# Two heads' retention projections as seven block products over half of the depth, woven into the attention projections, and a last slab that closes in two half banks

## What is computed

```
h = rms_norm(x);  p = h @ w_in                    # per head: retention q,k,v,gate and attention q,k,v
A = silu(gate) * group_norm(retention(rot(q), rot(k), v))         # 8 heads of 128
B = softmax(rms(q) @ rms(k).T + rel_bias) @ v                     # 8 heads of 128, chunk mask
x = x + concat(A, B) @ w_out
x = x + square(relu(rms_norm(x) @ w_ff1)) @ w_ff2
```

## Time and profile before

| | |
|---|---|
| median of 3 runs | 1113.13 us (1112.95 to 1113.15) |
| profiled execution: time / span | 1113.28 / 1111.2 us |
| busy: PE, PE weight loads | 1105.2 us (99%), 942.2 us (85%) |
| busy: DVE, ACT, POOL | 830.8 us (75%), 657.3 us (59%), 51.5 us (5%) |
| granted PE clock in 40 slices | 9 tenths or more in every slice |
| DMA | 253.14 MB, mean 228 GB/s |

### The profile page before, as it was taken

One profiled execution on the slowest core, in us unless ns is written; L12 is line 12 of the kernel. 1 busy time (PEld: TensorE's weight loads), 2 busy tenths in 40 slices (PEclk: granted clock), 3 DMA queues, 4 the chain that ended last, 5 costly groups with the idle time before them and its releaser, 6 DMA issues.

```text
span 1111.2 us, 13678 instructions
## 1 busy us (share of the span) xinstructions
PE 1105.2 (99%) x5234; PEld 942.2 (85%) x5234; DVE 830.8 (75%) x828; ACT 657.3 (59%) x765; POOL 51.5 (5%) x58
## 2 busy tenths in 40 slices
PE   9999999999999999999999999999999999999998
PEld 8889899899898888888888888888888888888887
DVE  6667566576576668869787869787869787869783
ACT  6544544554554556677655577665577665577662
POOL 0100000000000000000000000000000000000000
PEclk9999999999999999999999999999999999999999
DMA  9855455454464556787797787797787797787792
GB/s 362 319 191 180 151 198 179 151 197 153 156 217 152 204 208 182 266 278 220 246 290 222 258 277 221 243 291 221 259 279 220 244 291 221 259 277 219 246 278 86
DMA packets 39551, 253.14 MB, mean 228 GB/s; under 512 B 4432, under 2 KB 4944, under 8 KB 12624
## 3 DMA queue, kind: packets, MB, share of 16 engines
q1 hardware_dynamic: 34464, 218.12, 53.4%
q0 software_dynamic: 4608, 33.56, 16.0%
q10 hardware_dynamic: 432, 0.81, 0.2%
HBM read 250.37 MB, written 2.10 MB: 227 GB/s over the span
## 4 chain that ended last, share of the span: by engine, by line
PE 99%; DMA 0%; ACT 0%; DVE 0%; ACTq 0%; issue 0%
PE acc L489 11%; PE acc L496 11%; PE acc L503 11%; PE acc L667 10%; PE acc L665 10%; PE acc L663 10%; PE bankC L643 4%; PE acc L643 4%; PE acc L638 4%; PE bankC L638 4%; PE bankC L636 4%; PE acc L636 4%; PE bankD L643 1%; PE bankD L638 1%; PE bankD L636 1%; PE acc L687 1%
## 5 line engine op out<-in xcount | busy, mean ns | idle before, releaser
L1311 DVE TENSOR_TENSOR w_lo<-raw,w_hi 128x2048 fp32r<-128x2048 f32 x180 | 410.9, 2289 | 126.8 <-ACT w_hi L924 126.6
L924 ACT ACTIVATE w_hi<-raw 128x2048 fp32r<-128x2048 f32 x180 | 344.8, 1917 | 220.8 <-PE acc L667 145.9
L1118 DVE TENSOR_TENSOR w_lo<-raw,w_hi 128x1024 fp32r<-128x1024 f32 (+1 forms) x152 | 167.8, 1107 | 68.6 <-ACT w_hi L767 68.5
L767 ACT ACTIVATE w_hi<-raw 128x1024 fp32r<-128x1024 f32 (+1 forms) x152 | 142.9, 962 | 34.3 <-PE acc L503 25.3
L489 PE MATMUL acc<-w_hi,hT_hi 128*128 128x512 f32 (+1 forms) x512 | 129.5, 374 | 0.8 <-ACT w_hi L767 0.8
L496 PE MATMUL acc<-w_hi,hT_lo 128*128 128x512 f32 (+1 forms) x512 | 123.5, 362 | 0.0
L503 PE MATMUL acc<-w_lo,hT_hi 128*128 128x512 f32 (+1 forms) x512 | 123.2, 362 | 0.0
L496 PEld LDWEIGHTS acc<-w_hi,hT_lo 128*128 128x128 f32 x512 | 93.5, 188 | 10.5
L503 PEld LDWEIGHTS acc<-w_lo,hT_hi 128*128 128x128 f32 x512 | 93.4, 188 | 10.0
L663 PE MATMUL acc<-w_hi,hF_hi 128*128 128x512 f32 x256 | 100.8, 394 | 0.0
L663 PE MATMUL acc<-w_hi,dF_hi 128*128 128x512 f32 x256 | 99.9, 390 | 0.0
(11 more groups left out here) (187 smaller groups left out, 1573.4 us busy)
## 6 DMA issues: line engine op xcount, KB each, us to landing
raw<-in_w_up SPq DMA_DIRECT2D x64, 1024.0 KB, 6.4
raw<-in_w_down SPq DMA_DIRECT2D x64, 1024.0 KB, 6.5
raw<-in_w_ret SPq DMA_DIRECT2D x32, 1024.0 KB, 4.7
raw<-in_w_att SPq DMA_DIRECT2D x28, 768.0 KB, 4.4
raw<-in_w_out SPq DMA_DIRECT2D x16, 1024.0 KB, 4.7
raw<-in_w_up POOLq DMA_DIRECT2D x16, 1024.0 KB, 8.6
raw<-in_w_down POOLq DMA_DIRECT2D x16, 1024.0 KB, 8.9
raw<-in_w_att SPq DMA_DIRECT2D x6, 384.0 KB, 7.7
```

Source lines behind the costliest of these rows:

```text
L767: nc.scalar.activation(piece(w_hi, q, 0, PIECE_KT * n), raw[:, q // 2, (q % 2) * PIECE_KT * n:(q % 2 + 1) * PIECE_KT * n], ACT.Copy).then_ ...
L924: nc.scalar.activation(w_hi[:, ring(s)], raw[:, r, :], ACT.Copy).then_inc(slab_hi, 1)
L1118: nc.vector.tensor_tensor(piece(w_lo, q, 0, PIECE_KT * n), raw[:, q // 2, (q % 2) * PIECE_KT * n:(q % 2 + 1) * PIECE_KT * n], piece(w_hi, ...
L1311: nc.vector.tensor_tensor(w_lo[:, ring(s)], raw[:, r, :], w_hi[:, ring(s)].bitcast(f32), ALU.subtract).then_inc(slab_lo, 1)
```

## The change

**Projections.** The 16 groups become four blocks of two heads. A block has 19 steps of two pieces, in this order; `I` and `J` are the plain attention slabs of the two heads, the others are retention:

```diff
+STEPS = "I0 I1 I2 I3 J0 Q1 J1 P5 J2 P6 J3 P7 P3 Z1 Q2 Z2 P4 H1 H2".split()
+LOADS = "I0 I1 I2 I3 J0 a J1 b J2 d J3 Z1 e Z2 H1 H2".split()
```

```diff
+            def s_block(b):
+                nc.vector.tensor_tensor(s_blk[:, b, :]..., hT_hi[...], hT_lo[...], ALU.add).then_inc(s_blk_ok, 1)
...
+            at_piece(0, 8, s_first)
+            at_piece(0, 8, s_second)
+            at_piece(0, 9, s_third)
+            at_piece(0, 10, s_lo, 0)
+            at_piece(0, 11, s_lo, 1)
+            at_piece(0, 13, s_lo, 2)
+            at_piece(0, 15, s_lo, 3)
```

The weight combinations are made in every block: DVE adds slab b, and later d, to slot a, and POOL's accumulating DMAs add one more slab to b and to a. Banks are seeded from `in_p5`, `in_q1` and `bX`:

```diff
+            def in_sum(i, other, read):
+                nc.vector.tensor_tensor(raw[:, r, :], raw[:, r, :], raw[:, o[0], :], ALU.add).then_inc(in_summed, 1)
+            def set_z(i):
+                nc.vector.tensor_tensor(bZ[:], in_p5[:], bX[:], ALU.subtract).then_inc(z_set, 1)
+            def set_w(i):
+                dve.wait_ge(y_set, i + 1)
+                nc.vector.tensor_tensor(bW[:], in_p5[:], bX[:], ALU.subtract).then_inc(w_set, 1)
...
+                elif step == "Z1" and m == 1:
+                    pe.wait_ge(w_set, i + 1)
```

The small work gets new places (DVE's and PE's lists, cut; `h` is the even head of the block, `u` the even retention head; the odd retention head's work stands at pieces 1 to 7 of the next block, where `ret_work` had it):

```diff
+                at_piece(i, 10, att_mean_squares, h)
+                at_piece(i, 10, in_sum, i, "b", "Q1")
+                at_piece(i, 11, att_norm, h)
+                at_piece(i, 14, in_sum, i, "d", "P5")
+                at_piece(i, 20, set_z, i)
+                at_piece(i, 24, set_w, i)
+                at_piece(i, 24, att_mean_squares, h + 1)
+                at_piece(i, 25, att_norm, h + 1)
+                at_piece(i, 33, ret_rotate, u)
+                at_piece(i, 34, ret_rotated, u)
...
+                for h, first in ((2 * i, 12), (2 * i + 1, 26)):
+                    at_piece(i, first, att_T, h)
+                    at_piece(i, (18, 30)[h % 2], att_PT, h)
+                at_piece(i, 34, ret_T, 2 * i)
```

**Last slab.** In place of two banks of 512 columns, the second is closed in halves, the right one in `bX`:

```diff
+                for m, bank, first, end in ((0, bH, 0, N), (1, bY, 0, half), (1, bX, half, N)):
...
+                    right = xs[:, 1, c * N + half:(c + 1) * N]
+                    nc.vector.tensor_tensor(right, bX[:, half:N], right, ALU.add).then_inc(acc_read_dve, 1)
```

More of the change, by code:

```diff
@@ L175, in hybrid_block @@
         rope_in = sem("rope_in")
[L176 removed]
+        decay_in = [sem(f"decay_in{b}") for b in range(2)]
         xc_hi = sem("xc_hi")
@@ L605, in _ @@
+            for q in range(8 * G_OUT):
+                in_piece(q)
+                for f in work.get(q, ()):
+                    f()
+            work = {j: work.get(8 * G_OUT + j, []) for j in range(PIECES)}
             work[2] = work[2] + [lambda: pe.wait_ge(a_mix_lo, HEADS)]
+            work[3] = work[3] + [lambda: pe.wait_ge(r_mix_lo, HEADS - 2)]
+            work[6] = work[6] + [lambda: pe.wait_ge(r_mix_lo, HEADS)]
             def x_blocks(c):
@@ L645, in product, with last_slab @@
                 mm.then_inc(slab_used, 1)
+            def last_slab(p, step):
+                form = REST + (0 if place(p, step)[1] == 2 else MT)
+                s, half = slab_no(p, step), N // 2
+                pe.wait_ge(slab_lo, s + 1)
+                wh, wl = w_hi[:, ring(s)], w_lo[:, ring(s)]
+                for m, bank, first, end in ((0, bH, 0, N), (1, bY, 0, half), (1, bX, half, N)):
+                    for t in range(SLAB_KT):
+                        cols = slice(t * N + first, t * N + end)
+                        fresh = bank is bX and t == 0
+                        nc.tensor.matmul(bank[:, first:end], dF_hi[:, form + m, tile_cols(t)], wh[:, cols], start=fresh,
+                                         stop=False, skip_group_check=True)
+                        nc.tensor.matmul(bank[:, first:end], dF_hi[:, form + m, tile_cols(t)], wl[:, cols], start=False,
+                                         stop=False, skip_group_check=True)
+                        mm = nc.tensor.matmul(bank[:, first:end], dF_lo[:, form + m, tile_cols(t)], wh[:, cols],
+                                              start=False, stop=t == SLAB_KT - 1, skip_group_check=True)
+                    mm.then_inc((slab_used if bank is bX else half_used), 1)
             def rest(p, step, banks, closes=False, between=None):
@@ new lines, in _ @@
+            for q in range(8 * G_OUT):
+                nxt = q + AHEAD
+                if nxt < PIECES:
+                    x_hi(nxt)
+                if nxt < 8 * G_OUT:
+                    in_hi(nxt)
+                else:
+                    hi_piece(G_OUT, nxt - 8 * G_OUT, N)
+                if q == PIECES:
+                    act.wait_ge(gq_ok, 1)
+                for f in work.get(q, ()):
+                    f()
+            group(G_OUT, N, N, {j: work.get(8 * G_OUT + j, []) for j in range(PIECES)})
@@ L1296, in add_to_stream @@
+            for q in range(8 * G_OUT):
+                nxt = q + AHEAD
+                if nxt < PIECES:
+                    x_lo(nxt)
+                if nxt < 8 * G_OUT:
+                    in_lo(nxt)
+                else:
+                    lo_piece(G_OUT, nxt - 8 * G_OUT, N)
+                for f in work.get(q, ()):
+                    f()
+            group(G_OUT, N, N, {j: work.get(8 * G_OUT + j, []) for j in range(PIECES)})
             def add_to_stream(g, par, c):
+                dve.wait_ge(x_in[c], 32)
```

629 lines of the change are left out of this document (446 added, 183 removed).

## The result

The change takes 1133.87 us (1133.27 to 1134.24), against 1113.07 before in the runs made beside it: a ratio of 1.0186, 95% interval 1.0169 to 1.0204. It is slower, by 20.8 us. The forecast was 1134.

A forecast was written before the change was run, and what follows sets the result against it. PE's work was taken to bound the kernel, with DVE and ACT chains ending in its small work. 1113.28 - 10.0 + 31.1 - 0.3 = 1134.1, median 0.15 lower: 1134 us; 1125 to 1139 had 50%, stated range 1119 to 1142.

The forecast's parts named there:

- the last slab: End of the kernel: last slab's second bank as 24 matmuls of 256 columns, with smaller last addition and store; -0.3 us.
- PE's work: Retention of two heads takes 180 matmuls in place of 192, wide first matmuls dearer; -10.0 us net if PE never waits.
- Waits of blocks 1 to 3: PE waits for late DVE and ACT chains in each of these blocks: 1.5 + 0.3 + 1.2 + 0.6 + 2.1 = 5.7 us.
- 1.5, 1.2 and 2.1: PE's waits per block: 1.5 us at even head's `att_T`, 1.2 in Z1 and odd head's `att_T`, 2.1 at even head's `ret_T`.
- The two waits on `att_PT`: PE's waits at the transposes of the probabilities, per block: 0.3 us for the even head, 0.6 for the odd.
- Block 0: Combinations of h delay DVE: PE waits 8.7 us up to `a_qk`, 1.35 at `att_PT`, then the later waits; 14.0 us.
- the walk: Each engine's work followed in its own order with start-to-start times, to find PE's waits; 31.1 us in all.
- Rival (C): The clock falls to 1.2 GHz after block 0's two long waits, costing 5 to 7 us: 1140; chance 12%.
- a clock below 1.00 between 30 and 50 us: Sign in block 0 of the profile after, named as showing the forecast wrong and the clock rival right.
- (A): DVE and ACT run ahead, so the waits vanish and the count of matmuls decides: 1103 us; chance 7%.
- (B): Only block 0's opening wait is real, steady waits are absorbed: 1117 us, up to 1124; chance 15%.
- What was to cost nothing: Slab loads, POOL's accumulating loads (8.6 us, issued 15 us ahead), DMA share and second load of x: no PE wait.

The follow-up runs named there:

- the fill experiment: The changed kernel with 8 and 14 small matmuls on `ident`, which nothing reads, put on PE in block 0's two long waits: 1133.1 us.

## Why the forecast was right, step by step

**The account.** The front part was forecast at -10.0 + 31.1 = +21.1 us and is +21.8; the last slab at -0.3 and is -0.6. Blocks 1 to 3 are 88.19 - 85.23 = 2.96 longer each, 8.9 together, where 9.6 were forecast (88.6 - 85.4, three times); block 0 with what follows block 3 is the rest, 12.9, where 11.5 were forecast (14.0 - 2.5). These sum to 21.2 us of span, and the medians are 20.8 apart; the 0.4 between them is the spread of single runs and what the time has beyond the span (2.08 us before, 1.84 after). So the mechanism was right, the order of work on DVE and ACT, but that the total is right to 0.1 us is luck: sizes were off in opposite directions by up to 1.4 us.

**PE's work, -10.0: about 0.5 us a block too good.** With no listed wait left a period is 83.71 us, of which 0.5 are the two short waits shown above, and it was 85.23. So the change saves about 2.0 us of PE's time in each of blocks 1 to 3 and not 2.5: the term that was mis-sized most in proportion. A part of the difference is in the product pieces, which take 1.37 to 1.39 us in that trace (126.85 to 128.23, for one) where 1.36 was forecast; the rest is spread over many rows in hundredths. The base was off too: the sum took 85.40 for two heads where it is 85.23, but that stood on both sides of it.

**Waits of blocks 1 to 3, 5.7 each: they are 88.19 - 83.71 + 0.5 = 5.0.** Where the forecast had 1.5, 1.2 and 2.1, the moves that removed them took 0.3 (with a new wait in their place), 1.2 and 2.0 off the period. The two waits on `att_PT` (0.3 and 0.6) didn't show in the change's list. The even head's was behind the first wait, though: once `a_qk` was on time, `a_p` was 0.7 to 1.1 late in every block. The odd head's is the 0.22 above. One reading in the prediction is wrong and changes no term: ahead of `ret_T` in the kernel before there are three pieces of 2.08 behind `att_pv`, not four.

**Block 0, 14.0.** `att_T` was forecast 8.7 us late: 34.1 + 8.7 = 42.8, and it starts at 43.53. The two waits are where the walk put them (3.2 for `w_lo`, 3.9 for `a_qk`, each 0.2 to 0.3 more from start to start). `a_qk` idled 0.91 us for GpSimd's power, which took 4.46 here (rows in the last section) where the walk had counted on 2.19 from mean to `a_qk`: that is more than the 0.7. The 1.35 at `att_PT` isn't in the list; PE was late itself, by the lower clock.

**Rival (C), the clock, was right in its mechanism and too dear in its size.** It falls behind both waits: the windows above have 0.63 and 0.50 where PE works. The prediction named a clock below 1.00 between 30 and 50 us as a sign of being wrong. The sign came, and the time of 1140 didn't: it had 5 to 7 us for it. Behind the first wait it costs nothing, since PE then waits for `a_qk` anyway; behind the second it costs 2.2 us, of which the fill experiment got back 0.8. The forecast had nothing for that 0.8, so it is one of the terms by which block 0 came out longer. The Trainium skill (TensorE: Matmul & The Clock Gate, "HAM oscillation — how this bites in real kernels") states that idle gaps between bursts of matmuls bring half rate back; the trace after agrees, with a clock of 0.50 behind a gap of 3.85 us. Waits of up to 1.96 us (the fill experiment's) left the clock at 1.00.

**Rivals (A) and (B)** had ACT and DVE run ahead of PE. They don't: the steady waits are there, and moving the rotation alone gave 8.2 us. With the order mended the time is 1110.75, 7.8 over (A)'s 1103. What remains is 1.0 us in each block (83.71 where 85.23 - 2.5 = 82.7 was forecast), 3.9 together, and seven listed waits of 3.6 us, all in block 0 and before 51 us, with 0.2 to 0.3 more for each. These are estimates, and they add up to some 1.5 us more than the 7.8; 0.6 of that is the profiled execution, which was so much above the median.

**What was to cost nothing** did: PE waits for no transfer, while the accumulating loads take 9.5 us, not 8.6. One arrival is in the chain behind block 0's waits, as it was in the walk: slab `a` lands at 27.94 us, where the walk had 28.2.

**The last slab, -0.3: 0.6 to 0.75.** The matmuls are 0.12 us apart, as the slope of the rows had it. The addition takes 0.43 where it took 0.69. From its end to the end of the span it is 1132.4 - 1130.14 = 2.26 us, and was 1111.2 - 1108.33 = 2.87: 0.6 is saved behind the addition, where the store is half as large, and 0.15 was allowed.

## What to carry to other kernels

When work is taken from the engine that sets the time, walk every chain that ends in its small steps again: here some 8 us of matmul time went, and some 30 us of waits came (estimates from the account above), on engines that were 78% and 61% busy. If a walk in program order gives a wait at a given step, first try an earlier place for the operation that PE waits for, on the engine that is late: moves of some dozen lines, with no work removed, turned +20.8 us into -2.3. The one time that a consumer was moved later, it carried its own followers with it and gained 0.3 us.

## What the runs showed of the hardware that was not expected

GpSimd's power on 128x4 elements takes from 1.01 to 4.46 us, by what VectorE is doing when it starts. Timeline of the changed kernel in block 0 and block 1, then of the run with the probabilities a piece earlier:

```profile
37.94 2.28 DVE L1414 TENSOR_TENSOR raw<-raw 128x2048 f32<-128x2048 f32 x1
38.11 4.46 POOL L534 TENSOR_TENSOR a_rs<-a_ms,neg_half 128x4 f32<-128x4 f32 x1 [2.74 <-DVE a_ms L1481]
...
40.14 0.95 DVE L1405 TENSOR_TENSOR w_lo<-raw,w_hi 128x768 fp32r<-128x768 f32 x1
...
41.01 0.68 DVE L1451 TENSOR_TENSOR sf_lo<-s_mix,sf_hi 128x512 fp32r<-128x512 f32 x1
...
42.60 0.87 DVE L1488 TENSOR_SCALAR a_qk<-a_proj,a_rs 128x128 f32<-128x128 f32 x4 [0.91 <-POOL a_rs L534]
...
129.78 2.29 DVE L1414 TENSOR_TENSOR raw<-raw 128x2048 f32<-128x2048 f32 x1
129.96 2.98 POOL L534 TENSOR_TENSOR a_rs<-a_ms,neg_half 128x4 f32<-128x4 f32 x1 [8.61 <-DVE a_ms L1481]
...
131.98 0.95 DVE L1405 TENSOR_TENSOR w_lo<-raw,w_hi 128x768 fp32r<-128x768 f32 x1
```

```profile
120.07 1.01 POOL L534 TENSOR_TENSOR a_rs<-a_ms,neg_half 128x4 f32<-128x4 f32 x1 [7.00 <-DVE a_ms L1481]
120.55 0.96 DVE L1405 TENSOR_TENSOR w_lo<-raw,w_hi 128x768 fp32r<-128x768 f32 x1 [0.56 <-ACT w_hi L995]
```

In block 1 the power starts while the sum of two slabs runs, an operation with two inputs in SBUF, and ends at 132.94, 0.87 behind the sum's end (132.07). In the run above a `w_lo` with two inputs in SBUF starts half a microsecond behind the power, and the power takes its 1.01. The same holds for every such power in the traces of the kernel before, the change and six of the runs, but for one place: it ends 0.86 to 0.90 behind the end of the `w_lo` or sum that was running at its start, and takes 1.01 to 1.03 where none was. The place is block 0 with three such operations in a row. There it ends at 42.57, 0.88 behind the third (41.01 + 0.68 = 41.69) and not behind the first, while the second operation in block 1 and behind the power at 33.50 (rows above) didn't hold it. Why is open. The smaller powers on 128x2 elements take 0.71 us where VectorE is idle (27.19 us in the changed kernel), and 0.69 to 0.70 where an operation that reads PSUM is running at their start, as it is for all 24 of the retention heads in three of these traces.

The Trainium skill (SBUF — State Buffer, "SBUF: two separate sides") states that GpSimd and a VectorE operation with two SBUF inputs share a port pair, and that whichever starts first holds it for the whole instruction and blocks the other. The trace agrees for GpSimd. It does not show the other half: the `w_lo` at 120.55 starts beside a power and takes 0.96 us, where the `w_lo` at 131.98, which no power starts beside, takes 0.95. So in these kernels a small power in a chain was cheapest where VectorE was idle, or read PSUM, at the moment at which it started.
